# Starting the first layer of a two-layer trunk: first weight block loaded and rounded in halves, first two blocks and the loads and copies around them re-ordered

## What is computed

```python
c_act = jax.nn.silu(c)
for l in range(DEPTH):
    mod = (c_act @ w_mod[l] + b_mod[l])[:, None, :]
    sh1, sc1, g1, sh2, sc2, g2 = jnp.split(mod, 6, axis=-1)
    h = rmsnorm(x, norm1_g[l]) * (1.0 + sc1) + sh1
    proj = h @ w_in[l]
    q, k, v, ca, cb, su, gates = jnp.split(proj, [...], axis=-1)
    ...
    y_ssm = s5_ssm(su, ...)      # B and C matrices of 32 groups, 16 inputs, 64 states
    ...
    x = x + g1 * (mixed @ w_out[l])
    ...                          # then SwiGLU and a second residual add
```

## Time and profile before

| | us |
|---|---|
| median of the timed runs | 932.44 |
| profiled execution, its own time | 932.05 |
| its span, first to last instruction | 930.2 |
| TensorE busy | 902.1 |
| VectorE busy | 708.4 |
| ScalarE busy | 486.0 |

### The profile page before, as it was taken

How to read it: one execution, slowest core, us unless ns; L and a number is a source line. 1 busy time by engine, 2 the same in 40 slices (tenths; PEclk the granted TensorE clock), 3 DMA queues, 4 the chain that set the end, 5 groups by cost and what they waited for, 6 DMA issues and landing times.

```text
span 930.2 us, 15663 instructions
## 1 busy us (share of the span) xinstructions
PE 902.1 (97%) x6575; PEld 762.8 (82%) x6575; DVE 708.4 (76%) x941; ACT 486.0 (52%) x606; POOL 12.8 (1%) x13
## 2 busy tenths in 40 slices
PE   4999999999999999999999999999999999999996
PEld 1898977777778999899988998777777888888885
DVE  3896898899577688685777689989957766666666
ACT  4784248733647574645345325883473643343334
POOL 2000000000000000000000000000000000000001
PEclk9999999999999999999999999999999999999999
DMA  9993366657896559846876544446779455555531
GB/s 344 250 275 128 135 226 227 227 197 281 309 262 223 180 181 329 306 158 231 304 281 141 179 137 137 137 136 218 272 278 308 146 202 183 181 182 194 194 108 46
DMA packets 128565, 196.10 MB, mean 211 GB/s; under 512 B 30729, under 2 KB 90641, under 8 KB 122351
## 3 DMA queue, kind: packets, MB, share of 16 engines
q1 hardware_dynamic: 125815, 194.82, 62.6%
q10 hardware_dynamic: 2680, 0.29, 0.3%
HBM read 194.02 MB, written 1.06 MB: 210 GB/s over the span
## 4 chain that ended last, share of the span: by engine, by line
PE 82%; DVE 8%; ACT 3%; SPq 2%; DMA 2%; issue 2%; ACTq 1%; DVEq 0%
PE bank L613 19%; PE bank L615 18%; PE bank L614 18%; PE bank L979 8%; PE bank L980 4%; PE bank L651 3%; DVE wlo L1571 2%; PE bank L717 2%; DVE yc L1881 1%; SPq L587 1%; PE bank L741 1%; DMA raw<-in_w_in 1%; PE bank L729 1%; DMA ldt<-in_ssm_log_dt 1%; PE bank L899 1%
## 5 line engine op out<-in xcount | busy, mean ns | idle before, releaser
L1571 DVE TENSOR_TENSOR wlo<-raw,whi 128x2048 fp32r<-128x2048 f32 (+1 forms) x136 | 302.7, 2227 | 141.8 <-PE bank L615 68.4
L1172 ACT ACTIVATE whi<-raw 128x2048 fp32r<-128x2048 f32 x133 | 251.3, 1896 | 106.9 <-DMA raw<-in_w_in 53.3
L613 PE MATMUL bank<-hb,whi 128*128 128x256 f32 x592 | 170.1, 287 | 0.9 <-DVE wlo L1571 0.9
L614 PE MATMUL bank<-hb,whi 128*128 128x256 f32 x592 | 167.4, 283 | 0.0
L615 PE MATMUL bank<-hb,wlo 128*128 128x256 f32 x592 | 167.4, 283 | 0.0
L613 PE MATMUL bank<-whi,bhi 128*128 128x512 f32 x304 | 121.1, 398 | 0.3 <-DVE blo L1988 0.3
L979 PE MATMUL bank<-hb,whi 128*128 128x512 f32 x336 | 119.0, 398 | 0.0
L615 PE MATMUL bank<-whi,blo 128*128 128x512 f32 x304 | 118.7, 390 | 0.0
L614 PE MATMUL bank<-wlo,bhi 128*128 128x512 f32 x304 | 118.5, 390 | 0.0
L613 PEld LDWEIGHTS bank<-hb,whi 128*128 128x128 f32 x592 | 113.3, 191 | 3.5 <-DVE wlo L1571 1.3
L614 PEld LDWEIGHTS bank<-hb,whi 128*128 128x128 f32 x592 | 113.4, 192 | 0.4
(11 more groups left out here) (277 smaller groups left out, 1125.3 us busy)
## 6 DMA issues: line engine op xcount, KB each, us to landing
raw<-in_w_mod SPq DMA_DIRECT2D x48, 1024.0 KB, 5.6
raw<-in_w_ffn_in SPq DMA_DIRECT2D x44, 1024.0 KB, 5.1
raw<-in_w_in SPq DMA_DIRECT2D x38, 1024.0 KB, 7.0
raw<-in_w_ffn_out SPq DMA_DIRECT2D x22, 1024.0 KB, 5.0
raw<-in_w_out SPq DMA_DIRECT2D x8, 1024.0 KB, 7.5
raw<-in_w_in SPq DMA_DIRECT2D x16, 256.0 KB, 4.5
raw<-in_ssm_glu_b SPq DMA_DIRECT2D x4, 1024.0 KB, 6.3
raw<-in_ssm_glu_a SPq DMA_DIRECT2D x4, 1024.0 KB, 5.1
```

What stands on the lines that cost most here:

```text
L613: mm(o, w_hi, a_hi, start=start, stop=False, skip_group_check=True)
L614: mm(o, w_hi, a_lo, start=False, stop=False, skip_group_check=True)
L1172: fn(whi[mi % N_HI][:, n], raw[SLOT[item]][:, n], ACT.Copy).then_inc(hi_half if half == 0 else s_hi, 1)
L1571: part = V.tensor_tensor(wlo[mi % N_LO][:, n], raw[SLOT[("main", *divmod(mi, NB))]][:, n], whi[mi % N_HI][:, n].bitcast(F32), ALU.subtract)
```

## The change

Eight edits, all in the first layer's start:

1. `crow` (c), `ident` and `consts` are issued at the head of SyncE's queue, ahead of all of `w_mod`, no longer at the head of ScalarE's.
2. The loads of C and of B's real part move from before block 2's weights to before block 3's; the late constants and taps move from before block 3's to before block 4's.
3. Block 0's weights are loaded as two transfers of 512 KB, and rounded in two halves: half, two tiles of `norm_hi`, other half, six tiles. TensorE starts block 0 when the first half is rounded, and waits for the second at k = 4.
4. In block 0 the turning rounds 0 and 1 are taken out. Block 1 gets an order of its own: all products with the high weights, then rounds 0 and 1, then the products with the low weights.
5. ScalarE's doubling of C, the copies of rounds 0 and 1 and `b_spread(0, 0)` move behind `hi(2)` and the copy of block 0's result; `b_spread(0, 0)` now stands before `hi(3)`.
6. `b_source(0, 1)` moves from i = 0 to i = 1 on VectorE, so behind `lo(3)`.
7. Rounds 6 and 7 move from t = 7 to t = 8, rounds 8 and 9 from t = 8 to t = 9 (on both engines).
8. The last `keep_busy` before block 0 has 7 matmuls in place of 17. One wait of layer 1 counts one more (`hi_half`).

```diff
-ROUND_AT = [{5: (2, 3), 6: (4, 5), 7: (6, 7), 8: (8, 9)}, {2 * (PREP_AT + 5 + n) + 1: (n,) for n in range(ROUNDS)}]
+ROUND_AT = [{5: (2, 3), 6: (4, 5), 8: (6, 7), 9: (8, 9)}, {2 * (PREP_AT + 5 + n) + 1: (n,) for n in range(ROUNDS)}]
-B_SPREAD_AT = [{0: 0, 2: 1}, {PREP_AT + 6: 1}]
+B_SPREAD_AT = [{2: 1}, {PREP_AT + 6: 1}]
...
         def _(sp):
+            sp.dma_start(crow[:, :], A["c"].rearrange("b (r c) -> (b r) c", c=P)).then_inc(s_c, 16)
+            sp.dma_start(ident[:, :], A["c_ident"]).then_inc(s_const, 16)
+            sp.dma_start(consts[:, :], A["c_small"]).then_inc(s_const, 16)
...
-                if item == ("main", 0, 2):
+                if item == ("main", 0, 3):
                     load_c(sp, 0)
                     load_b(sp, 0, 0)
-                if item == ("main", 0, 3):
+                if item == ("main", 0, 4):
                     late_constants(sp)
                     load_taps(sp, 0)
...
+                    if item == ("main", 0, 0):
+                        ((d, src),) = main(0, 0, dst)
+                        sp.dma_start(d[:, 0:4], src[:, 0:4]).then_inc(s_first, 16)
+                        sp.dma_start(d[:, 4:8], src[:, 4:8]).then_inc(landed, 16)
...
-                if mi:
+                if mi == 1:
+                    pe.wait_ge(s_hi, 2)
+                elif mi:
                     pe.wait_ge(s_lo[lo_engine(i)], LO_NO[(l, i)] + 1)
                 else:
-                    pe.wait_ge(s_hi, 1)
+                    pe.wait_ge(hi_half, 1)
...
+                        if mi == 0 and k == 4:
+                            pe.wait_ge(s_hi, 1)
...
-                        for r in range(2):
-                            prep_round(0, r)
...
+                elif mi == 1:
+                    o = unit_bank(l, i)
+                    for k in range(DK):
+                        for c in range(2):
+                            for a in (hhi, hlo):
+                                mm(o[:, c * T:(c + 1) * T], w8[0][:, k, c * P:(c + 1) * P], a[:, k, :], start=(k == 0 and c == 0 and a is hhi), stop=False,
+                                   skip_group_check=True)
+                    for r in range(2):
+                        prep_round(0, r)
+                    middle()
+                    pe.wait_ge(s_lo[lo_engine(i)], LO_NO[(l, i)] + 1)
+                    for k in range(DK):
+                        for c in range(2):
+                            last = mm(o[:, c * T:(c + 1) * T], w8[1][:, k, c * P:(c + 1) * P], hhi[:, k, :], start=False, stop=(k == DK - 1),
                                       skip_group_check=True)
                     last.then_inc(s_unit, 1)
...
-            keep_busy(bank[0], 17)
+            keep_busy(bank[0], 7)
...
-                act.wait_ge(s_land[SLOT[item]], LANDED[item])
+                if mi == 0 and half == 0:
+                    act.wait_ge(s_first, 16)
+                else:
+                    act.wait_ge(s_land[SLOT[item]], LANDED[item])
...
-            act.dma_start(crow[:, :], A["c"].rearrange("b (r c) -> (b r) c", c=P)).then_inc(s_c, 16)
-            act.dma_start(ident[:, :], A["c_ident"]).then_inc(s_const, 16)
-            act.dma_start(consts[:, :], A["c_small"]).then_inc(s_const, 16)
...
-            hi(0)
-            norm_hi(0, 0, DK)
+            hi(0, 0)
+            norm_hi(0, 0, 2)
+            hi(0, 1)
+            norm_hi(0, 2, DK)
             hi(1)
-            act.wait_ge(s_cc[0], 32)
-            fn(once[:, :, 1, :], once[:, :, 0, :], ACT.Copy).then_inc(c_twice, 1)
-            for n in range(2):
-                round_copy(0, n)
...
+                    if (l, i) == (0, 1):
+                        act.wait_ge(s_cc[0], 32)
+                        fn(once[:, :, 1, :], once[:, :, 0, :], ACT.Copy).then_inc(c_twice, 1)
+                        for n in range(2):
+                            round_copy(0, n)
+                        b_spread(0, 0)
...
-                    if (l, i) == (0, 0):
+                    if (l, i) == (0, 1):
                         b_source(0, 1)
```

More of the change, by code:

```diff
@@ L400, in trunk @@
         hi_half = sem("hi_half_ready")
+        s_first = sem("first_half_landed")
         s_lo = {"pool": sem("lo_ready_pool"), "dve": sem("lo_ready_dve")}
@@ L585, in _ @@
                         load_taps(sp, 1)
-                    for d, src in main(item[1], item[2], dst):
-                        sp.dma_start(d, src).then_inc(landed, 16)
+                    if item == ("main", 0, 0):
[3 more added lines that the diff above has]
+                    else:
+                        for d, src in main(item[1], item[2], dst):
+                            sp.dma_start(d, src).then_inc(landed, 16)
                     if item[1] == 0 and DEPTH > 1 and item[2] == AT[("fg", 0)]:
@@ L911, in main_block @@
                             last = mm(o[:, c * T:(c + 1) * T], w8[0][:, k, c * P:(c + 1) * P], hlo[:, k, :], start=False, stop=(k == DK - 1),
+                                      skip_group_check=True)
+                    last.then_inc(s_unit, 1)
+                elif mi == 1:
[4 more added lines that the diff above has]
+                                mm(o[:, c * T:(c + 1) * T], w8[0][:, k, c * P:(c + 1) * P], a[:, k, :], start=(k == 0 and c == 0 and a is hhi), stop=False,
+                                   skip_group_check=True)
+                    for r in range(2):
[5 more added lines that the diff above has]
+                            last = mm(o[:, c * T:(c + 1) * T], w8[1][:, k, c * P:(c + 1) * P], hhi[:, k, :], start=False, stop=(k == DK - 1),
                                       skip_group_check=True)
@@ L1564, in lo @@
                 if half == 0 and mi == NB + 1:
-                    dve.wait_ge(hi_half, 1)
+                    dve.wait_ge(hi_half, 2)
                 else:
```

## The result

| | before | after |
|---|---|---|
| median of the timed runs, us | 931.62 (930.68 to 933.60) | 934.34 (933.13 to 936.64) |
| runs | 19 | 19 |
| ratio of the medians, 95% interval | | 1.0027 [1.0020, 1.0033] |
| profiled execution, its own time, us | 932.05 | 933.30 |
| its span, us | 930.2 | 931.5 |

The change makes the kernel slower by 0.27%, 2.7 us. The profiled execution took 933.3, the figure that was predicted for the median; the median lies 1.0 above it, inside the range. The two need separate reasons. So there is a part of some 1.7 us that each execution pays, and a part of 0.7 to 3.3 us more that comes and goes. The forecast had 0.9 for the first and 0.03 of a chance for the second.

The account below looks back on a forecast made before the run. TensorE, busy 902.1 of 930.2 us, was taken as the bound. Start gains caught by VectorE's list and a new wait summed to 0.9 later: 932.05 plus 0.9, plus 0.39 for the median, gives 933.3 us, range 930.8 to 935.8.

Parts of the forecast that it names:

- the sum: First layer, first matmul behind block 4: 75.6 to 75.7 against 74.79, so 0.9 us later, taken as the end's shift.
- The case with most of the chance: Whole kernel: time stays the same within 0.2% (1.9 us) of before; chance 0.64.
- The stage before block 0: Loads and weight stream up to the first `h` tile: taken as 0, bounds 1.5 us later to 2.6 earlier.
- the gain of the filled dip: Transfers between 18 and 20 us, at 193 GB/s against 412: filling this gap saves 1.06 us.
- Halves and block 0: Block 0's start: the 4.18 us wait for its weights goes; first matmul near 32.3; splitting costs ScalarE nothing.
- The new chain: ScalarE's and VectorE's lists from rounds 0 and 1 to round 6's copy at 69.6: TensorE waits some 2 us before rounds 8 and 9.
- chain not binding: Rival, rounds 8 and 9: round 6's copy comes in time, so 1.3 us faster than before, 931.1; chance 0.11.
- The early gain caught by `lo(2)`: Block 2's start: `lo(2)` on VectorE unchanged, so TensorE, 1.4 us ahead, starts at 48.15, only 0.6 ahead.
- Loads: C, B and blocks 2 and 3 land just in time: cost 0; rival of late loads, 934.8 to 936.1, chance 0.16.
- Filler matmuls are free, since PE waits for the first tile anyway: Before block 0: leaving out fillers costs nothing, as TensorE waits for the first tile until about 32.2.
- Nothing behind it is edited, and I take a shift there as the shift of the end: Behind block 4: the shift of the first matmul there, 74.79 before, passes unchanged to the kernel's end.
- The clock: Rival: the new 2 us wait or missing fillers slow TensorE's clock for one block, some 5 us, 938; chance 0.03.

Follow-up runs that it names:

- consts_only: Kernel before with only c, `ident` and `consts` put at the head of SyncE's queue: 931.89 us, 1.0002 of before.
- copies_first: Kernel after, with ScalarE's copies of rounds 6 and 7 put ahead of `c_spread(0, 0)`: 931.99 us, 0.9997 of before.
- b_source_back: Kernel after, with `b_source(0, 1)` put ahead of `lo(3)` on VectorE again: 931.64 us, 0.9993 of before.
- keep7_only: Kernel before with only the last `keep_busy` before block 0 cut from 17 to 7 matmuls: 933.43 us, 1.0019 of before.
- keep7_moved: Kernel before with 7 fillers ahead of block 0 and the other ten at the head of TensorE's list: 932.51 us, 1.0005 of before.
- after_again: Kernel after, unedited, timed again beside other kernels: 933.44 us, 1.0014 of before.
- rounds_back: Kernel after with edit 7 undone, rounds 6 and 7 at t = 7, 8 and 9 at t = 8: 933.99 us, 1.0024 of before.
- fill_waits: Kernel after with 5 fillers added before block 2 and 6 before rounds 8 and 9: 932.84 us, 1.0006 of before.
- combined: Kernel after with the edits of copies_first, b_source_back and fill_waits together: 932.28 us, 1.0002 of before.
- after_moved: Kernel after with ten fillers added at the head of TensorE's list: 937.13 us over six executions, 1.0049 of before.
- source_back_filled: b_source_back with five fillers at the head of TensorE's list and five before block 2: 931.97 us, 1.0002 of before.

## Why the prediction was right, and where it was not

**Its time: right, in part by luck.** Forecast 933.3 in a range of 930.8 to 935.8; measured 934.34 once and 933.44 once more. The sign of the sum, +0.9, was right, its size was not: the medians differ by 2.7 and by 1.5. The figure came out near because the three runs that it started from had a median of 932.44, 0.8 above that of the nineteen (931.62). And the profiled execution's +1.3 has another make-up than the forecast's +0.9: 0.49 from the chain that was reckoned with, and 0.8 from a place that was put at nothing. The case with most of the chance, within 0.2% of before, is not where the first comparison ended (0.27% [0.20%, 0.33%]); the second is inside it (0.14% [0.06%, 0.22%]).

**The stage before block 0: taken as 0, came as -0.86.** This is the term of the sum that was mis-sized. I had let the gain of the filled dip (1.06) and the loss of the three issues (1.5) cancel. The dip filled as forecast (434 GB/s), but the following 8 us also ran at 402 in place of 377, and the stream came out ahead. consts_only shows that edit 1 alone gives 0.62 of it.

**Halves and block 0: right.** First matmul forecast 32.3, measured 31.72, early by the stage. The second half of the weights was rounded at 31.88 with no wait for its transfer. So the two transfers of 512 KB cost nothing that these rows show. The Trainium skill (DMA: Bandwidth & Descriptors, Bandwidth) asks for 1 MiB or more, and the prediction had read from it that the second half would land late; it did not, and the measurement decides. What the halves are worth by themselves was not run: the earlier start of block 0 ends at block 2 in any case.

**The new chain: right in every link.** `lo(3)` forecast 51.9, measured 51.45; VectorE's idle time before it 3.7, measured 3.15; wait at rounds 8 and 9 2, measured 1.50; milestone 75.6, measured 75.28. The 0.4 between is that of the chain's start: rounds 0 and 1 began at 43.99, not 44.5. copies_first and b_source_back each remove the wait and bring the milestone to 73.7. One remark beside the chain was a wrong reading: the 0.7 of the earlier trace rows is put down to the copies of rounds 6 and 7, but it stood before round 6, for the copy of round 4. The chain does not use it. The rival *chain not binding* does, and fairly: without a wait before the turning rounds, copies_first and b_source_back are 1.07 and 1.09 ahead of before at the milestone, where it had 1.3.

**The early gain caught by `lo(2)`: right, for another reason than given, so by luck.** I had `lo(2)` unchanged because its inputs and its queue are. It did start at 46.01 (45.94 before), but what set that was B: VectorE was through with `lo(1)` 1.13 ahead of B's landing at 42.47, and `b_source(0, 0)`, 3.5 long, and `lo(2)` stand behind it. Two errors met: VectorE was 0.86 ahead by the stage before, and B held it up. Block 2: forecast 48.2, measured 48.35, released by `wlo`.

**Loads: cost 0 at the milestone, but with a wrong deadline.** B was forecast for 43.9 and needed, I wrote, by 44.2. It landed at 42.47 and was needed at 41.3, because `lo(2)` stands behind `b_source(0, 0)` on VectorE. At the milestone nothing came of it while the wait at rounds 8 and 9 was there to take it up. In b_source_back, where that wait is gone, the 1.09 that VectorE idles for B lies on the path. Block 2's weights were rounded at 40.59 (39.7 forecast). An earlier load of B was not tried.

**"Filler matmuls are free, since PE waits for the first tile anyway": the step that failed.** They were free to run, but not free to leave out. keep7_only, with nothing else changed, is 1.0019 [1.0009, 1.0029]. With the ten put back at the head of the list (keep7_moved) it is 1.0005 [0.9997, 1.0014].

**"Nothing behind it is edited, and I take a shift there as the shift of the end": failed as well.** The part behind the milestone is 855.4 us before and 856.2 after, in a stretch whose instructions are the same. The last column of the table sorts cleanly: in the six profiled executions of kernels whose list ahead of layer 1's `ssm_in` has ten matmuls fewer than before (after, after_again, copies_first, b_source_back, keep7_only, rounds_back) it is 856.2 to 857.3; in the others (before, consts_only, fill_waits, combined and the four with fillers at the head), 855.4 to 855.9. All of the former show gaps put down to issue there, 0.56 to 0.84 behind the 104th matmul or 0.67 at 516.92, and none of the latter. That the gap depends on how many instructions stand ahead on TensorE's list is shown by keep7_only against keep7_moved.

The traces also tell what may lie behind it. Their DMA records hold, beside the data, packets of 16 KB on a queue of the kind `instruction`, as many in every kernel; here kernel after, whole span (packets, MB, share of 16 engines):

```profile
q8 instruction: 52, 0.85, 0.4%
```

In the eight kernels without a gap in layer 1, one of these packets starts 0.3 to 0.8 us ahead of the 128 small matmuls (before: 518.44, matmuls from 518.90). In the six with a gap there it starts 0.7 to 1.6 us behind the first of them (after: 520.43 against 519.38; keep7_only: 520.49 against 519.33). And every gap named above ends 1.2 to 1.6 us after such a packet has ended: after's two at 516.43 and 523.08, with packets until 514.84 and 521.51. The same is so of the third wait in the result section's view, the gap of 0.8 to 1.4 us at about 86 us, in all fourteen kernels (before: packet until 84.46, matmuls go on at 85.91). So these gaps go with the loading of instructions, and ten matmuls more or fewer ahead move the loading to another place of the work. Most packets have no gap behind them; that TensorE runs out of instructions there, and that the queue is TensorE's, is inferred.

**The clock.** I had it as a rival at 0.03, worth 5 us, "if the new 2 us wait or the missing fillers bring that back". Profiled executions have both: the fall at 34.9 us behind the missing fillers (keep7_only) and that at 71.3 behind the new wait (after_moved). There is a third place, in layer 1 behind the issue gap (after_again, copies_first). The first can't be set down to the kernel after: there block 0 begins at 31.72, right behind the last filler, and no wait of that kind is left. The price was too high: half of a stretch of 3.4 us is 1.7 lost on TensorE, half of one of 6.8 is 3.4, and I had reckoned with the work of a whole block, 5.8 us, at half speed. At the end less arrives where a later wait takes it up: about 0.8 in after_again, and 0.23 at the milestone in keep7_only. The chance was far too low: eleven of nineteen executions of the kernel after lie below the mean clock of the other eight.

**The sum as measured.** +0.49 at the milestone and +0.8 behind it give the span's +1.3. The profiled execution of before was itself 0.4 above its median, so that the eight executions of after at the higher clock (933.1 to 933.5) lie some 1.7 above before's median. The other eleven lift the median by another 1.0, to 934.34.

**What stays open.** The timed executions have no trace, so where the clock fell in the longer ones of the kernel after is not known; that it fell is read from their mean clock. The other kernels narrow it down. Of the 47 executions of copies_first, b_source_back, fill_waits and combined, in which TensorE does not idle before a turning round, none has a mean clock below 0.997 and none took over 933.11. Of the 39 of after, after_again and rounds_back, which keep such a wait, eleven are below 0.997. copies_first and b_source_back have the gap in layer 1 as after has, and the wait before block 2. So the large losses go with the wait before the rounds more than with the others. It is a tendency and no proof: source_back_filled has one execution of eleven at 0.996, the kernel before two of 94 in the later comparisons, and there is no trace of an execution of after that took over 935 us.

Fillers at the head of the list delay the last `w_mod` block by 0.9 to 1.6 us: its matmuls begin at 28.49 to 29.84 with five or ten of them, against 27.45, 27.63 and 28.32 in after, b_source_back and before. In these four kernels the first 16 KB packet of instructions starts at 26.0 to 26.6, while that block is being loaded; in the ten others it starts at 28.2 to 29.6, when the block has landed. That the packet is what delays the block fits these times; it was not tested.

## What to carry to other kernels

Before taking away work that hides in a wait, ask what it does besides waiting: here ten unread matmuls filled a wait behind which the clock fell once they were gone (in the kernel before), and they set where the later instructions stand in the engine's list. In the profiled executions the missing ten cost 0.8 us far behind the edit, more than the 0.49 that the whole reordering cost at the milestone. Follow a moved operation on each engine's queue to the next cross-engine hand-over; the chain through ScalarE's and VectorE's lists gave the new wait's place and size to half a microsecond. And do not take the shift at a milestone for the shift of the end: compare the time behind the milestone as well, across several variants.

## What the runs showed of the hardware

- A gap in TensorE's stream with no wait behind it (0.56 to 0.84 us) comes and goes half a millisecond after the edit, with the number of matmuls ahead of it: there with ten fewer, gone with the same number or one more. In each of the fourteen traces such gaps end 1.2 to 1.6 us after a 16 KB packet of the instruction queue, also the one at about 86 us that all kernels have (0.8 to 1.4 us).
- The granted clock of a TensorE that is busy for 97% of the span still falls to its half level, for 3.4 or 6.8 us, behind waits of 1.83 (keep7_only) and 2.47 us (after_moved), and in two profiled executions behind 128 matmuls on 32 rows with a gap of 0.84 or 0.56 us in them. It does so in some executions and not in others: the profiled execution of after had a wait of 1.50 and a gap of 0.56 and kept its clock, and b_source_back's kept it through a gap of 0.83.
- Small transfers at the head of the queue paid for themselves: TensorE's first work, which waits for `consts`, began at 3.54 us in place of 9.39, and the weight stream behind them was 0.87 us ahead by its last block.
